# Two gaps in on-chip memory: where the split weights and the feed-forward activations of a four-layer fp32 stack begin

## What is computed

```python
def first_block(x, ...):
    for l in range(DEPTH):                       # DEPTH = 2, D_MODEL = 1024, D_FF = 2816
        h = rmsnorm(x, ffn1_norm[l])
        x = x + 0.5 * swiglu(h, ffn1_w_gate[l], ffn1_w_up[l], ffn1_w_down[l])
        h = rmsnorm(x, mix_norm[l])
        p = h @ w_in[l]
        ...
        y = jnp.concatenate([y_pool, y_four, y_attn], axis=-1) @ w_out[l]
        x = x + y
        h = rmsnorm(x, ffn2_norm[l])
        x = x + 0.5 * swiglu(h, ffn2_w_gate[l], ffn2_w_up[l], ffn2_w_down[l])
    return rmsnorm(x, final_norm)

def swiglu(x, w_gate, w_up, w_down):
    return (jax.nn.silu(x @ w_gate) * (x @ w_up)) @ w_down
```

## Time and profile before

| | before |
|---|---|
| median of 3 runs | 2531.75 us (2531.56 to 2534.13) |
| span of the profiled execution | 2529.9 us |
| TensorE busy | 2457.5 us, 97% |
| VectorE, ScalarE, GpSimd busy | 45%, 43%, 44% |
| mean granted TensorE clock | 0.993 of full |

### The profile page before, as it was taken

The page is one execution under the profiler, slowest core; times in us unless marked ns, Lnnn a source line. Parts: engine busy times, 40 slices in busy tenths (PEclk is TensorE's granted clock), DMA queues, the critical chain, the costliest instruction groups (busy, mean ns, idle before and its releaser), DMA issues.

```text
span 2529.9 us, 30096 instructions
## 1 busy us (share of the span) xinstructions
PE 2457.5 (97%) x10934; PEld 1924.6 (76%) x10934; DVE 1134.4 (45%) x1780; ACT 1082.3 (43%) x1584; POOL 1122.4 (44%) x828
## 2 busy tenths in 40 slices
PE   8999999989999999999999989999999998999988
PEld 6888888667888888888888668888887665676666
DVE  5444115564444105444025655444136655465553
ACT  4333124454333214333132544333125777357772
POOL 4554445415455445554445414554445232352323
PEclk9999999999999999999999999999999999999999
DMA  4222223202222222222223203222233222122212
GB/s 172 85 97 99 100 88 128 84 34 100 99 99 88 95 100 92 91 99 99 100 83 129 73 32 110 90 98 99 100 119 104 83 80 67 67 96 75 84 63 83
DMA packets 37528, 233.17 MB, mean 92 GB/s; under 512 B 5184, under 2 KB 5312, under 8 KB 10816
## 3 DMA queue, kind: packets, MB, share of 16 engines
q1 hardware_dynamic: 36000, 226.51, 25.9%
q10 hardware_dynamic: 1440, 5.45, 0.6%
HBM read 223.55 MB, written 2.10 MB: 89 GB/s over the span
## 4 chain that ended last, share of the span: by engine, by line
issue 58%; POOL 41%; POOLq 1%
POOL w_lo L437 41%; POOLq L431 0%; POOLq L435 0%; POOLq L212 0%; POOLq L437 0%; POOLq L1874 0%
## 5 line engine op out<-in xcount | busy, mean ns | idle before, releaser
L437 POOL TENSOR_TENSOR w_lo<-raw,w_hi 128x512 fp32r<-128x512 f32 x824 | 1122.2, 1394 | 1406.9 <-ACT w_hi L924 1406.8
L445 PE MATMUL ps<-h_hi,w_hi 128*128 128x512 f32 x2304 | 921.3, 400 | 14.0 <-DVE h_lo L1330 7.9
L447 PE MATMUL ps<-h_hi,w_lo 128*128 128x512 f32 x2304 | 900.3, 391 | 0.0
L446 PE MATMUL ps<-h_lo,w_hi 128*128 128x512 f32 x2304 | 899.2, 390 | 0.0
L924 ACT ACTIVATE w_hi<-raw 128x1024 fp32r<-128x1024 f32 x412 | 413.3, 1052 | 881.2 <-PE ps L447 877.0
L445 PEld LDWEIGHTS ps<-h_hi,w_hi 128*128 128x128 f32 x2304 | 434.5, 189 | 115.7 <-issue 13.8
L446 PEld LDWEIGHTS ps<-h_lo,w_hi 128*128 128x128 f32 x2304 | 434.6, 189 | 93.5 <-issue 6.0
L447 PEld LDWEIGHTS ps<-h_hi,w_lo 128*128 128x128 f32 x2304 | 433.7, 188 | 92.2
L447 PE MATMUL ps<-hid_hi,w_lo 128*128 128x512 f32 x704 | 278.1, 395 | 0.0
L445 PE MATMUL ps<-hid_hi,w_hi 128*128 128x512 f32 x704 | 278.1, 395 | 0.0
L446 PE MATMUL ps<-hid_lo,w_hi 128*128 128x512 f32 x704 | 278.1, 395 | 0.0
(11 more groups left out here) (236 smaller groups left out, 2083.6 us busy)
## 6 DMA issues: line engine op xcount, KB each, us to landing
raw<-in_stream SPq DMA_DIRECT2D x206, 1024.0 KB, 4.8
hraw<-xs SPq DMA_DIRECT2D x96, 64.0 KB, 2.0
x_sb<-in_x SPq DMA_DIRECT2D x4, 512.0 KB, 10.5
out_x<-x_sb SPq DMA_DIRECT2D x8, 256.0 KB, 2.7
mem_sb<-in_mem ACTq DMA_DIRECT2D x1, 1024.0 KB, 10.2
rec_sb<-in_recip ACTq DMA_DIRECT2D x2, 512.0 KB, 4.6
memn<-in_mem ACTq DMA_DIRECT2D x1, 1024.0 KB, 4.8
dist_sb<-in_dist ACTq DMA_DIRECT2D x2, 448.0 KB, 3.1
```

Of the source, the lines that this page charges most:

```text
L437: gp.tensor_tensor(w_lo[:, s, c], raw[:, s, c], w_hi[:, s, c].bitcast(F32), ALU.subtract).then_inc(lo_split, 1)
L445: pe.matmul(dst, l_hi, r_hi, start=first, stop=False)
L446: pe.matmul(dst, l_hi, r_lo, start=False, stop=False)
L447: return pe.matmul(dst, l_lo, r_hi, start=False, stop=last)
```

## The change

It adds 16 unused elements (64 bytes) behind each slot of `w_hi` and of `w_lo`, and an unused tensor of 96 elements (384 bytes) behind `w_lo`. The views that the kernel uses keep their shape.

```diff
+W_GAP = 16
+HID_GAP = 96
...
         raw = sb("raw", [P, 2, PANEL])
-        w_hi = sb("w_hi", [P, 2, PANEL], F32R)
-        w_lo = sb("w_lo", [P, 2, PANEL], F32R)
+        w_hi = sb("w_hi", [P, 2, PANEL + W_GAP], F32R)[:, :, 0:PANEL]
+        w_lo = sb("w_lo", [P, 2, PANEL + W_GAP], F32R)[:, :, 0:PANEL]
+        sb("hid_gap", [P, HID_GAP])
         cst = sb("cst", [P, NC])
```

## The result

The changed kernel takes 2559.32 us (median of 4 runs, 2554.83 to 2560.14) against 2531.65 us of the kernel before (4 runs beside it). The ratio is 1.0103, with a 95% interval from 1.009 to 1.0115. The forecast was 2517.5 us, with a range up to 2550: it failed in the sign. The price of rival 1, 2558 us, is within 2 us of what came.

A forecast was written before the change was run, and what follows sets the result against it. TensorE, busy 97% of the span, was taken as the bound: matmul count times step between starts. (a) 14.1 us less, (b) 0 and (c) nothing took the span from 2529.9 to 2515.8, the median to 2517.5 us; range 2493 to 2550.

The forecast's parts named there:

- rival 1: Gate/up and down matmuls: equal load-stream offset is best, so shifted weights cost 6.6 ns each; 2558 us, chance 0.27.
- (b): Shifted weight slots in 512-column matmuls: cost unknown in sign, 4608 odd-slot matmuls may lose or gain 30.4 us; taken as 0.
- (a): Down stretches: hid moves to the offset of h, so 2112 matmuls fall from 233.3 to 226.7 ns, 14.1 us less.
- (c): Buffers behind hid (cst, sq, ms and others) move together by 640 bytes; costed at nothing.
- fixed part of 13.3 ns: Gate/up step of 226.7 ns: what each matmul carries beyond one cycle per column, sized from the 256-column stage's 120 ns.
- Rival 2: Down stage: hid's address isn't what makes it slow, so nothing changes; 2531.75 us, chance 0.13.
- Rival 3: Odd weight slots: new distances beat the equal one, gate/up gains 30.4 us more; 2487 us, chance 0.20.

The follow-up runs named there:

- b_wgaps: Against the kernel before: only the gaps behind the weight slots, hid left at offset 0 modulo 512; 2560.57 us, ratio 1.0108.
- a_hid: Against the kernel before: only hid moves, by 640 bytes to offset 128 modulo 512, weights stay; 2518.18 us against 2534.1, ratio 0.9942.
- c_slot: Against the kernel before: 64 bytes between slots, w_hi and w_lo alike within a slot (128, then 192), hid at 128; 2545.83 us, ratio 1.0049.
- k_hid384: Against the kernel before: only hid moves, by 384 bytes, to 256 bytes from the weights modulo 512; 2519.77 us against 2532.73, ratio 0.9954.
- h_plus16: Against the kernel before: slot 1 of both weights at 112, slot 0 and h at 128, hid at 384; 2517.38 us (one run).

## Why the prediction was wrong

**The failed step is (b)**: of the shifted weights the prediction says "I take 0 in the middle, for want of a row". They cost 26.5 us: b_wgaps, which has them alone, takes 2560.57 us against 2534.1. On top of (a), as in the change, they cost more: 2559.32 us against 2518.18 of a_hid, 41.1 us. That is beyond the 30.4 us at which the prediction bounded the loss, since it counted only the odd slots; in the long stretches the even ones lose as much, 4.9 ns a step (231.6 against 226.7). The row for it was there: the only distance in the trace of before, the down stage, was the slow one. I used it for (a), as a loss to be taken away, and not for (b), where the same loss was put onto the larger stage. Rival 1 did so and had the right time.

**(a) was right in itself and didn't come in the change.** hid alone gives 119.68 us a down stretch where 119.7 was said: 14.0 us in the four, where 14.1 was counted (the medians differ by 15.9 us, the spans by 13.6). In the changed kernel down only falls to 231.6 ns (3.6 us in all), since the weights have left the offset to which hid came. I added (a) and (b) as if they were apart; they share an operand.

**Rival 1 was right in sign and size, and its rule too simple.** It let each mismatched load cost 6.6 ns and no more. c_slot bears this out to 0.6 ns. But with w_lo alone apart two steps in three are long, and with h_lo alone apart all three. By its rule the changed kernel's odd panels should have 233.3 ns and its even ones 228.9; they have 231.5 to 231.7 alike. The sum came out right because the two errors, 1.7 ns too much and 2.7 too little, largely cancel; in that part its good price was luck.

**What bounds the kernel** was read rightly: all of the difference is in the distance between matmul starts, with no wait in it, and the other engines followed at every pace. (c) was right as well: all matmuls but those with h or hid as the stream take 1.6 us more together, 1.0 of it where w streams past h, which is a matter of (b). The start was counted modulo 512; k_hid384 shows that 256 is enough. The fixed part of 13.3 ns isn't fixed either: with 256 columns the step went down from 120 to 113.3 ns (last section).

**The rivals.** Rival 2 is out by a_hid, and the rule behind it with it. The Trainium skill, SBUF — State Buffer, "Who interferes with whom", has TensorE never wait on anyone, with independent ports for stream and load. In these stretches it waits on no other engine, but the step still depends by 6.6 ns on where its own two reads stand to each other. Rival 3 is out for 512 columns and the distances tried. It holds in the small stage with 256 columns, where the changed kernel gains 0.6 us.

**What stays open.** That the loss comes from TensorE's reads of stream and weights is shown by moving each of them alone, and by the step being the same with the other engines idle. What they collide on, why two of three steps or all three are long where one operand in three is apart, why +64 has a pace of 228.9 ns and -64 none seen below 233.3, and what chooses between the paces at one distance: none of that was tried. No version beats equal offsets by more than runs differ (h_plus16, one run, has 2517.38 us): hid moved by 640 bytes and the weights left alone, 2518.18 us, is 0.6% faster than the kernel before and 1.6% faster than the changed one (2559.32 / 2518.18 = 1.016).

## What to carry to other kernels

Where matmuls follow each other without waits, divide the length of such a stretch by its count and compare stretches of the same shape; a few ns of difference at one clock is worth a look at the addresses. Here, for matmuls of 512 columns, all split operands, those that stream and those that are loaded, belong at the same offset modulo 256 bytes, and gaps between them have to be multiples of 256. A change of one operand's address has to be priced against every stage that uses that operand, with the slow row as the price, before a gain in another stage is counted.

## What the runs showed of the hardware beyond what was expected

A matmul with 512 columns in fp32r has a step of 226.7 ns when all its operands start alike modulo 256 bytes, and 228.3 to 234.2 ns at the other distances in most stretches. A stream at an unequal distance can hold one of several paces for hundreds of matmuls: at -16, 233.3 ns in three feed-forward parts and 226.7 in the fourth; at +16, 226.7 in the first and 228.3 in three; at +64, 233.3 in one and 228.9 in three. The pace passes over from gate/up to down without a break. With 256 columns the relation is another: equal offsets aren't the best. In a_hid, with all operands alike, those matmuls take 120 ns a step, and in the kernel before, at a distance of 128, 118.6 ns in the first such stretch and 120 in the second. In the changed kernel the panel in slot 1, whose w_hi and w_lo stand 64 bytes from the stream to either side, has 113.3 ns. Six steps each, first in a_hid (0.72 us), then in the changed kernel (0.68 us):

```profile
1892.95 0.28 PE L447 MATMUL ps<-mh_lo,w_hi 128*128 128x256 f32 x1
...
1893.67 0.28 PE L447 MATMUL ps<-mh_lo,w_hi 128*128 128x256 f32 x1
...
1928.98 0.28 PE L449 MATMUL ps<-mh_lo,w_hi 128*128 128x256 f32 x1
...
1929.66 0.28 PE L449 MATMUL ps<-mh_lo,w_hi 128*128 128x256 f32 x1
```
